# The last gate load as 120 and 8 partitions, and a later store of the first 128 tokens

## The reference

```python
h = h + mixed @ w_out[i]
h = h + peer_ffn(rmsnorm_2(h, ffn_norm[i]), peer_wq[i], peer_keys[i], peer_u[i], peer_v[i])
gate = jax.nn.sigmoid(rmsnorm_2(h, ple_gate_norm[i]) @ ple_gate_w[i])
h = h + (p[i] @ ple_proj[i]) * gate
```

## Time and profile before

| | |
|---|---|
| median of 3 runs | 1087.12 us (1086.24 to 1088.46) |
| profiled execution, its own time | 1087.19 us |
| its span | 1085.4 us |
| granted TensorE clock, mean | 0.986 |
| TensorE matmul / weight load busy | 993.2 / 566.4 us |
| VectorE / ScalarE / GpSimd busy | 688.2 / 460.3 / 317.2 us |
| DMA moved | 347.31 MB, mean 320 GB/s |
| of it gathers (queue 0) / SyncE's and other plain DMAs (queue 1) | 269.89 / 76.69 MB |

### The profile page before, as it was taken

One profiled execution on the slowest core, in us unless ns is written; L12 is line 12 of the kernel. 1 busy time (PEld: TensorE's weight loads), 2 busy tenths in 40 slices (PEclk: granted clock), 3 DMA queues, 4 the chain that ended last, 5 costly groups with the idle time before them and its releaser, 6 DMA issues.

```text
span 1085.4 us, 11222 instructions
## 1 busy us (share of the span) xinstructions
PE 993.2 (92%) x3773; PEld 566.4 (52%) x3773; DVE 688.2 (63%) x1555; ACT 460.3 (42%) x1201; POOL 317.2 (29%) x307
## 2 busy tenths in 40 slices
PE   9998999999999999999899698998788988877878
PEld 8998668444795565644454253555333432222324
DVE  5879556223553489787686676766458668667553
ACT  1253356111363157554644534445254364344333
POOL 4000000010000044445454334353434544443430
PEclk9999999999999999999999899999899999999999
DMA  9434442334627279999999999999999999999990
GB/s 354 169 135 186 155 155 78 123 118 167 242 90 309 103 295 421 421 415 422 422 420 421 421 420 422 420 421 421 422 421 420 421 422 413 421 422 420 418 416 33
DMA packets 46827, 347.31 MB, mean 320 GB/s; under 512 B 5073, under 2 KB 6481, under 8 KB 9265
## 3 DMA queue, kind: packets, MB, share of 16 engines
q0 software_dynamic: 37584, 269.89, 60.1%
q1 hardware_dynamic: 9184, 76.69, 18.6%
HBM read 345.25 MB, written 1.05 MB: 319 GB/s over the span
## 4 chain that ended last, share of the span: by engine, by line
PE 54%; DMA 29%; DVE 9%; ACT 6%; issue 2%; POOL 0%; DVEq 0%; POOLq 0%; ACTq 0%
DMA xc_rg<-in_peer_uv,small 20%; PE pp L1206 16%; PE pp L752 5%; DMA tail<-in_peer_uv,small 4%; PE pp L748 4%; PE pp L710 3%; DMA ig<-in_peer_uv,small 3%; PE pp L879 3%; PE pp L669 3%; PE pp L857 3%; PE pp L899 3%; DMA spare<-in_peer_uv,small 2%; PE pp L1096 2%; PE pp L706 2%; PE pp L1318 2%
## 5 line engine op out<-in xcount | busy, mean ns | idle before, releaser
L1681 ACT ACTIVATE small<-small 128x1 f32<-128x1 f32 x256 | 51.6, 202 | 319.0 <-DVE small L2462 318.0
L1695 ACT ACTIVATE diag<-ident,small 128x128 f32<-128x128 f32 x256 | 102.8, 402 | 8.4
L1206 PE MATMUL pp<-gl,diag 128*128 128x512 f32 x128 | 65.6, 637 | 21.2 <-ACT diag L1695 21.1
L1687 ACT ACTIVATE small<-small 128x1 f32<-128x1 f32 x256 | 75.4, 294 | 9.3
L1206 PE MATMUL pp<-sm,diag 128*128 128x512 f32 x128 | 64.3, 624 | 11.3 <-ACT diag L1695 11.3
L1206 PE MATMUL pp<-ig,diag 128*128 128x512 f32 x128 | 63.6, 620 | 10.1 <-ACT diag L1695 10.1
L1206 PE MATMUL pp<-kT,diag 128*128 128x512 f32 x128 | 63.4, 618 | 9.1 <-ACT diag L1695 9.1
L1206 PE MATMUL pp<-xc_rg,diag 128*128 128x512 f32 x128 | 61.6, 604 | 10.3 <-ACT diag L1695 10.3
L621 POOL DMA_INDIRECT ig<-in_peer_uv,small x32 | 40.2, 1257 | 105.0 <-PE pa L1161 53.6
L1206 PE MATMUL pp<-tail,diag 128*128 128x512 f32 x128 | 61.7, 604 | 9.1 <-ACT diag L1695 9.1
L1206 PE MATMUL pp<-spare,diag 128*128 128x512 f32 x128 | 62.7, 613 | 7.5 <-ACT diag L1695 7.5
(11 more groups left out here) (556 smaller groups left out, 2028.3 us busy)
## 6 DMA issues: line engine op xcount, KB each, us to landing
ring<-in_wall SPq DMA_DIRECT2D x31, 2048.0 KB, 7.9
ring<-in_wall SPq DMA_DIRECT2D x3, 512.0 KB, 7.0
ring<-in_wall SPq DMA_DIRECT2D x1, 1280.0 KB, 9.6
xs<-in_x SPq DMA_DIRECT2D x2, 512.0 KB, 3.7
post_g<-in_rows POOLq DMA_DIRECT2D x2, 512.0 KB, 8.5
tail<-in_wall SPq DMA_DIRECT2D x1, 1024.0 KB, 10.8
kT<-in_wall SPq DMA_DIRECT2D x1, 1024.0 KB, 12.8
lt<-in_sub_keys SPq DMA_DIRECT2D x1, 1024.0 KB, 8.2
```

Of the source, the lines that this page charges most:

```text
L1206: return nc.tensor.matmul(acc[t][:, c, :], diag[:, n * P:(n + 1) * P], rows_uv[page_of(g)][:, D + c * HALF:D + (c + 1) * HALF], start=Fals ...
L1681: nc.scalar.activation(acts[:, at:at + BATCH], dots[:, at:at + BATCH], ACT.Gelu_apprx_tanh)\
L1687: ins = nc.scalar.activation(wk[:, g % LAG:g % LAG + 1], acts[:, g % LAG:g % LAG + 1], ACT.Copy, scale=probs[:, g:g + 1])
L1695: nc.scalar.activation(diag[:, n * P:(n + 1) * P], ident[:, :], ACT.Copy, scale=wk[:, g % LAG:g % LAG + 1]).then_inc(s["diag_made"], 1)
```

## The change

`gw1` is loaded by two DMAs, the first for partitions 0 to 119, the second for partitions 120 to 127. `LOAD_OF` counts both, so that users wait for both. Before the first of the output's stores SyncE waits until both last pieces have landed (`piece_here`); the two stores of the first 128 tokens, issued so far when `y_made` allowed them, come behind this wait.

```diff
-LOAD_OF = [sum(ring_slot(v) == ring_slot(u) for v in range(1, u + 1)) for u in range(len(UNITS))]
+ROW_RANGES = {"gw1": ((0, 120), (120, P))}
+LOAD_OF = [sum(len(ROW_RANGES.get(UNITS[v], (P,))) for v in range(1, u + 1) if ring_slot(v) == ring_slot(u))
+           for u in range(len(UNITS))]
...
-                    sp.dma_start(places[:, :, HALF_OF[name], :], wall[u].rearrange("p (s n) -> p s n", s=2))\
-                        .then_inc(unit_ready[ring_slot(u)], 16)
+                    for n, m in ROW_RANGES.get(name, ((0, P),)):
+                        sp.dma_start(places[n:m, :, HALF_OF[name], :], wall[u][n:m].rearrange("p (s n) -> p s n", s=2))\
+                            .then_inc(unit_ready[ring_slot(u)], 16)
                     continue
...
             parts = [(0, 0, HALF), (0, HALF, D)] + [(1, a, b) for a, b in LAST_PARTS]
+            for n in range(LAST):
+                sp.wait_ge(piece_here[n], 16)
             for n, (t, a, b) in enumerate(parts):
```

## The result

The changed kernel takes 1096.62 us (median of 4 runs, 1094.45 to 1097.79) where the kernel before took 1087.62 us (1086.24 to 1088.46). The ratio is 1.0082, 95% interval 1.006 to 1.0104: 9 us slower, where 2.4 us faster was forecast and 1087.0 was the upper end of the range. The profiled execution took 1094.45 us, its span is 1092.7 us, 7.3 us over that of before.

A forecast was written before the change was run, and what follows sets the result against it. The prediction took the gathers' DMA, at the end its latest engine, to bound the kernel; 1.2 us from the split and 1.2 us from the stores, 2.4 us off 1087.12, gave 1084.7 us, range 1083.6 to 1087.0.

The forecast's parts named there:

- What bounds the kernel: Second half and end of the kernel: the gathers' DMA sets the pace, 2.49 us a slot; the end follows the latest engine.
- The stores: Two 256 KB output stores moved from 898 us to behind the last pieces: 1.2 us gained, bounds 0 and 2.2.
- The split: Load of `gw1` as 120 and 8 rows: one engine spared, the end gains 1.2 us, cut by the next engine.
- bounds of plus and minus 4.98 us: `gw1` load, latest engine: relieved by 4.98 us, or charged 4.98 us if all 8 rows go to it and it isn't relieved.
- The slower rival: Small DMA near 765 us: the 8 rows fall on the latest, unrelieved engine, 3.8 us slower, 1090.9 us; chance 0.09.
- the assumption of equal shares: `gw1` load: 120 rows keep shares of 8, so fifteen engines carry them and one carries none.
- the forecast's other half: End of the gathers: the spared engine is the latest one, so its 1.5 us alone at share 0.06 goes or falls below 0.6.
- the rival of another relieved engine: `gw1` load: the spared engine isn't the latest, only the stores' 1.2 us remain, 1085.9 or 1086.5 us; chance 0.28.
- theory P: From the even/odd run, not the prediction: engines take four successive rows, crowding groups, so that load is slow, 1092 to 1097 us.

## Why the prediction was wrong

**What bounds the kernel** was read rightly. The gathers' DMA time set the time; what changed it (9.56 us at the loads, 1.27 at the stores) moved the span one for one: the last landing went from 1063.8 to 1071.2, 7.4 us, the span by 7.3.

**The stores** were right in kind and size: 1.2 us forecast, 1.27 in the dots, and ratios of 0.9989 and 0.9984 alone. They went out at 1071.76, behind the last piece, at no cost that shows.

**The split** is the step that failed, at the sentence that relieves one engine by 4.98 us and charges 0.62 us for a row dealt again. Its term was a gain of 1.2 us; the split alone measured a loss of 9.9 us (9.56 us in the dots of the changed kernel). The sum priced bytes per engine at 26.3 GB/s whatever partitions they went to. That pace came from DMAs of 128 partitions alone, the only kind in the rows. My bounds of plus and minus 4.98 us "of what the latest engine sees" took it as fixed. In the runs the pace itself changes with the shape: 2 MB cost 4.8 us undivided, 12.2 us for 120 of the rows, 2.8 us for the other 8. I had no term for a load whose packets, and the gathers' beside them, take longer: 0.53 and 0.60 us for 8 KB in place of 0.31. The measured 1096.6 us lies beyond the slowest rival too, 1090.9.

**The slower rival** had the right sign and the wrong mechanism. It put the 8 rows on one engine, for 3.8 us. The count of small packets shows them on eight, and the 120 rows carry the larger part.

**Which engine was spared.** Fifteen engines took the 120 rows, so the assumption of equal shares was right. But the latest stands alone at the end for the same 1.5 us as before, so the forecast's other half fell too: on this point the rival of another relieved engine was right. It follows, though no run shows it, that even a full-speed load of this kind would have gained nothing beyond the stores.

**The rules that I had read.** The rule of the Trainium skill (DMA: Bandwidth & Descriptors, Rules for kernel authors) on dividing transfers, which I let count as "no gain", has the right direction and is too mild here: a division by columns, or by even and odd rows, costs nothing, one by neighbouring partitions 7 to 10 us. The ports of the Trainium skill (SBUF — State Buffer, Door 1: The DMA port swizzle) I didn't weigh. They fit the half rate of the 64 partitions and the cost of the 8, and they don't account for the 120.

**Open.** Why 120, 112 and 60 rows are slow although they reach every group isn't settled. One reading: theory P's sharing, each engine with rows that follow each other, would crowd the groups for 120 and 60 rows. But it would for 64 even rows too, so that count would have to be shared in another way. That they are not shared as 128 or 64 are is only argued: 64 even partitions run at 423 GB/s, 60 odd ones at 231 to 280. The packets' engines aren't named in the trace, so neither their rows nor the name of the latest engine can be read. One rival is untested throughout: partitions side by side are also rows side by side in `wall`, the source, and every run that changed the one changed the other. The 197 GB/s fit the ports of SBUF in the Trainium skill (SBUF — State Buffer, Door 1: The DMA port swizzle), but no run here moves the same source rows to other partitions.

## What to carry to other kernels

A DMA into SBUF is priced by its partitions before its bytes: keep the 128, or a strided half of them, and divide by columns if it must be divided. A price per byte read from full-width transfers holds for full-width transfers; once a change alters the shape, the price of the old shape is not a bound. A DMA that only has to be done by the end is worth its bytes when it moves out of a DMA-bound stretch, here 1.2 us for 0.5 MB.

## What the runs showed of the hardware

- Eight partitions side by side (128 KB) cost 2.8 us in the gathers' stream, eight apart (0 to 28) nothing that shows.
- A slow transfer slows everything on its engines: for 15 us load and gathers together ran at 220 to 254 GB/s with a busy share of 1.01 to 1.09, and 8 KB of a gather took 0.60 us in place of 0.31. The busy share can't tell it, only the GB/s beside it.
- The count of small packets tells how many engines a DMA used: 551 packets against 544 here (15 + 8 in place of 16).
